# Scores padded to 128 rows with zeros, nearer softmax steps in one layer, and a key projection placed ahead of an output projection

## The reference, cut to what matters

```python
# layer A, one chunk: the stabilizer m_t enters every decay
d = b[..., :, None] - b[..., None, :] + ib[..., None, :]
m_t = jnp.maximum(inter, jnp.max(d, axis=-1))
p = jnp.einsum("bhtd,bhsd->bhts", qb, kb) * jnp.exp(d - m_t[..., None])
# layer B: a head has 128 columns without and 64 with rotary position
QK_HEAD = QK_NOPE + QK_ROPE        # 128 + 64
# the cross attention of the second block
kv = (mem_n @ w_ckv).reshape(B, M, 2, CROSS_HEADS, CROSS_HEAD_DIM)
s = jnp.einsum('bshd,bmhd->bhsm', q, k) * CROSS_HEAD_DIM ** -0.5
```

## Time and profile before

| | |
|---|---|
| median of 3 runs | 1611.77 us (1610.45 to 1612.25) |
| the profiled execution | 1605.89 us, span of its records 1604.1 us |
| instructions | 19197 |
| TensorE busy | 1552.2 us, 97% |
| mean granted clock of TensorE | 0.993 of full speed |

### The profile page before, as it was taken

One profiled execution on the slowest core, in us unless ns is written; L12 is line 12 of the kernel. 1 busy time (PEld: TensorE's weight loads), 2 busy tenths in 40 slices (PEclk: granted clock), 3 DMA queues, 4 the chain that ended last, 5 costly groups with the idle time before them and its releaser, 6 DMA issues.

```text
span 1604.1 us, 19197 instructions
## 1 busy us (share of the span) xinstructions
PE 1552.2 (97%) x7128; PEld 1239.7 (77%) x7128; DVE 890.2 (55%) x1775; ACT 705.5 (44%) x1607; POOL 192.1 (12%) x157
## 2 busy tenths in 40 slices
PE   7999999999999999999899999999999999999997
PEld 5887777777897877766478878688777888888886
DVE  6467485656465567556448557664455534444343
ACT  6544353333355666555334444442344333333241
POOL 3202020202120000000014004320001100000001
PEclk9999999999999999999999999999999999999998
DMA  5522122323424222121123321234322333333321
GB/s 191 158 74 72 53 80 66 92 66 118 125 67 143 81 62 61 49 71 42 40 79 120 92 67 55 65 105 120 99 84 79 95 103 93 101 96 93 105 93 65
DMA packets 89068, 141.04 MB, mean 88 GB/s; under 512 B 6416, under 2 KB 36496, under 8 KB 88976
## 3 DMA queue, kind: packets, MB, share of 16 engines
q1 hardware_dynamic: 88256, 139.02, 28.5%
q10 hardware_dynamic: 720, 0.81, 0.1%
HBM read 137.71 MB, written 2.10 MB: 87 GB/s over the span
## 4 chain that ended last, share of the span: by engine, by line
PE 78%; DVE 9%; ACT 5%; issue 3%; POOL 3%; DMA 2%; SPq 0%; POOLq 0%; ACTq 0%; DVEq 0%
PE banks L1242 16%; PE banks L1244 16%; PE banks L1243 16%; PE banks L1247 6%; PE banks L1249 6%; PE banks L1248 6%; PE banks L1205 2%; DVE sb_w_split L1927 2%; DVE sb_arena L1936 2%; ACT sb_junk L1512 2%; PE banks L1420 1%; PE banks L1405 1%; PE banks L1368 1%; ACT sb_w_split L1544 1%; DVE sb_arena L1927 1%
## 5 line engine op out<-in xcount | busy, mean ns | idle before, releaser
L1927 DVE TENSOR_TENSOR sb_w_split<-sb_raw,sb_w_split 128x512 fp32r<-128x512 f32 (+4 forms) x530 | 338.7, 681 | 359.8 <-ACT sb_w_split L1544 359.1
L1544 ACT ACTIVATE sb_w_split<-sb_raw 128x512 fp32r<-128x512 f32 (+4 forms) x530 | 288.2, 592 | 425.3 <-PE banks L1244 309.5
L1242 PE MATMUL banks<-sb_actA,sb_w_split 128*128 128x512 f32 x672 | 275.7, 410 | 0.3 <-ACT sb_arena L1604 0.3
L1244 PE MATMUL banks<-sb_actA,sb_w_split 128*128 128x512 f32 x672 | 262.7, 391 | 0.0
L1243 PE MATMUL banks<-sb_actA,sb_w_split 128*128 128x512 f32 x672 | 261.8, 390 | 0.0
L1242 PE MATMUL banks<-sb_actB,sb_w_split 128*128 128x512 f32 (+1 forms) x640 | 248.8, 389 | 4.2 <-DVE sb_actB L1927 2.2
L1244 PE MATMUL banks<-sb_actB,sb_w_split 128*128 128x512 f32 (+1 forms) x640 | 242.9, 379 | 0.0
L1243 PE MATMUL banks<-sb_actB,sb_w_split 128*128 128x512 f32 (+1 forms) x640 | 242.7, 379 | 0.0
L1247 PE MATMUL banks<-sb_w_split,sb_actA 128*128 128x512 f32 (+1 forms) x384 | 153.5, 400 | 12.6 <-DVE sb_w_split L1927 9.2
L1249 PE MATMUL banks<-sb_w_split,sb_actA 128*128 128x512 f32 (+1 forms) x384 | 149.3, 389 | 0.0
L1248 PE MATMUL banks<-sb_w_split,sb_actA 128*128 128x512 f32 (+1 forms) x384 | 149.0, 388 | 0.0
(11 more groups left out here) (206 smaller groups left out, 2061.4 us busy)
## 6 DMA issues: line engine op xcount, KB each, us to landing
sb_raw<-in_a_w_in SPq DMA_DIRECT2D x66, 256.0 KB, 3.0
sb_raw<-in_w_up SPq DMA_DIRECT2D x32, 512.0 KB, 3.6
sb_raw<-in_w_down SPq DMA_DIRECT2D x32, 512.0 KB, 3.7
sb_raw<-in_w_in SPq DMA_DIRECT2D x24, 512.0 KB, 3.6
sb_raw<-in_mem_w_kv SPq DMA_DIRECT2D x16, 512.0 KB, 3.8
sb_raw<-in_w_ckv SPq DMA_DIRECT2D x16, 512.0 KB, 3.7
sb_raw<-in_a_w_in SPq DMA_DIRECT2D x15, 512.0 KB, 3.8
sb_raw<-in_a_w_out SPq DMA_DIRECT2D x12, 512.0 KB, 3.9
```

The costliest lines, as they stand in the source:

```text
L1242: pe.op.matmul(out, hi[:, cs], x.hi(k), start=i == 0, stop=False)
L1244: t = pe.op.matmul(out, lo[:, cs], x.hi(k), start=False, stop=last_i)
L1544: act.op.activation(hi[:, cs], raw[:, cs], ACT.Copy).then_inc(act.mark(m("w_hi"), 2 * n + part + 1), 1)
L1927: dve.op.tensor_tensor(out, a, b, op).then_inc(dve.mark(*mark) if mark else dve.tick(), 1)
```

## The change

- `asc` and `hsc` take all 128 partitions. The rotary query of a head gets a tile of its own (`q_pe`), whose other half GpSimd sets to zero (in `prep4`); the stabilizer rows become 128 rows (`m_rows`), set to zero ahead of time, and the selector is used with its 128 rows. ScalarE copies the rotary queries in two halves.
- `mla` has `lag=1300`, `mem_b` `lag=1300, wait=1000`.
- `prep4` of the last pair comes only after the split of mixer tile 3, and the evictions of zB3 wait for the scores of head 3, since the new tiles lie where these were.
- ckD0 moves from behind outC1 to ahead of outC0; its result moves in the arena, and its evictions wait for the last pooling step. `dho` comes one group later, the loop has one group more, and cqD0 starts row by row.

```diff
--- before.py
+++ after.py
@@ -646,11 +646,11 @@
         rounds(0, [(h, j) for h in (h0, h0 + 1) for j in range(TT)], "asc", "atp",
                lambda u: [("aval", *u), ("ysplit", "yB", *u)], [("prep6", h0 // 2)],
                lambda u: [("silu", f"zB{u[0] // 2}", u[0] % 2)] + ([("ev", "quB3", 3)] if u[0] == B_HEADS - 1 else []),
-               lag=1400, wait=1000)
+               lag=1300, wait=1000)
 
     def mem_b(h0):
         rounds(0, [("B", h, i) for h in (h0, h0 + 1) for i in range(TT)], "msc", "mtp", lambda u: [("mval", *u)],
-               [("hnscale", "mqB"), ("hnt", "mk1", 3)], [("silu", f"mzB{h0 // 2}", 1)], lag=1600, wait=1200)
+               [("hnscale", "mqB"), ("hnt", "mk1", 3)], [("silu", f"mzB{h0 // 2}", 1)], lag=1300, wait=1000)
 
     def latents(q):
         if q == 3:
@@ -659,7 +659,8 @@
         p.need(("lat", "qlT", 2))
         p.product(f"quB{q}", [("prep6", q - 1)] if q else [])
         for n in range(7):
-            p.side(1, [("asc", 2 * q - 3, TT - 1)] if q >= 2 and n == 0 else (), (f"prep{n}", q), lag=4000 if n in (0, 6) else 2600)
+            after = [("asc", 2 * q - 3, TT - 1)] if q >= 2 and n == 0 else [("ysplit", "yB", 3)] if (q, n) == (3, 4) else ()
+            p.side(1, after, (f"prep{n}", q), lag=4000 if n in (0, 6) else 2600)
 
     def gated(name):
         p.product(name, (), lambda j: [(("silu", name, j),)])
@@ -708,7 +709,7 @@
     p.product("vC")
     units = [(h, j) for h in range(DIFF_HEADS) for j in range(TT)]
     turned, closing = None, []
-    for n in range(len(units) + 8):
+    for n in range(len(units) + 9):
         group, after, split = [], [("rtp", "q", 3)] if n == 0 else [], []
         for parts in closing:
             if len(parts) > 1:
@@ -720,7 +721,7 @@
             if turned[1] == TT - 1:
                 h = turned[0]
                 after = [("gateG", "gC4")]
-                closing.append([[("dhs", h)], [("dhr", h)], [("dho", h)], [("ysplit", "yC", 4 + h)]])
+                closing.append([[("dhs", h)], [("dhr", h)], [], [("dho", h)], [("ysplit", "yC", 4 + h)]])
             turned = None
         if 2 <= n < len(units) + 2:
             turned = units[n - 2]
@@ -742,17 +743,17 @@
         p.side(1, [("gateG", "gC0"), ("nrow", "m2"), ("dsc", g, TT - 1)], ("pp", g), *([("ysplit", "yC", g - 1)] if g else []))
     p.side(1, (), ("ysplit", "yC", POOL_GROUPS - 1))
     p.product("gC0", (), lambda j: [(("gateG", "gC0"),)] if j == 3 else [])
+    p.product("ckD0", [("nrow", "m2"), ("pw", POOL_GROUPS - 1)])
     p.product("outC0", first=False)
     p.product("outC1")
 
 
     p.put(("enter", "outC1"))
     scales(0, "d", after=[("sqp", "d", 7)])
-    p.product("ckD0")
     p.product("ckD1")
     p.rings = [(4, 5), (6, 7)]
     for g in range(2):
-        p.product(f"cqD{g}", [("nrow", "d")])
+        p.product(f"cqD{g}", [("nrow", "d")], first=g > 0)
         for n in (2 * g, 2 * g + 1):
             rounds(n % 2, [(n, i) for i in range(TT)], "csc", "ctp", lambda u: [("cval", *u)], (),
                    [("ev", f"cvD{g}", MT - 1)])
@@ -875,8 +876,8 @@
         self.decay = at.take(2, SEQ)
         self.u_pad = at.take(4, CONV_W + SEQ)
         self.sigA = at.take(2, SEQ)
-        self.neg_m = self.arena[0:4, at.at:at.at + SEQ]
-        at.take(SEQ)
+        self.m_rows = at.take(SEQ)
+        self.neg_m = self.m_rows[0:4, :]
         self.y_tok = at.take(TT, M_DIM)
         flat = self.y_tok.rearrange("p a b -> p (a b)")
         self.gate_f = flat[:, 0:SEQ]
@@ -918,6 +919,8 @@
         self.v_pair = [at.take(TT, 2 * V_HEAD) for _ in range(3)]
         self.kpe = at.take(TT, QK_ROPE)
         self.zT = [two[:, 1, 0:2, :], at.take(2, SEQ), two[:, 1, 4:6, :], Layout(self.arena, ARENA - 2048).take(2, SEQ)]
+        other = [self.zT[3][:, 0, :], self.zT[3][:, 1, :], two[:, 0, 6, :], self.zT[1][:, 0, :]]
+        self.q_pe = [[self.peT[n % 2][:, 1, :], other[n]] for n in range(4)]
         mprob_b = two[:, 0, 0:2, :].rearrange("p a b -> p (a b)")
         self.pair_pe = Layout(self.arena, ARENA - 1024).take(2, TT, 2 * QK_ROPE)
         self.sigB = self.cons[:, CON["head_rows"]:CON["head_rows"] + SEQ].rearrange("p (a b) -> p a b", a=1)
@@ -967,9 +970,9 @@
         self.row["m2"] = self.cons[:, CON["head_rows"]:CON["head_rows"] + N_MEM]
         self.scratch["m2"] = two[:, 0, 3, 0:N_MEM + P]
         at = Layout(self.arena, N_LATE + SEQ + 8 * SEQ + 4 * SEQ + 4 * SEQ)
+        self.cqT = at.take(8, SEQ)
         self.ckT = at.take(KD, N_MEM)
         self.cv = at.take(MT, D_MODEL)
-        self.cqT = at.take(8, SEQ)
         self.cpT = [at.take(MT, SEQ), at.take(MT, SEQ)]
         at = Layout(self.arena)
         self.cprob = [at.take(3, N_MEM), at.take(3, N_MEM)]
@@ -1347,8 +1350,8 @@
             place, full = open_bank(step)
             pe.wait_ge(*m.emptied(("gateT",)))
             mb = v.bank(place, n=n)
-            pe.op.matmul(mb, v.con("head_rows", h * P, (h + 1) * P, M_HEADS), v.neg_m[:, si * P:SEQ],
-                         start=True, stop=False)
+            pe.wait_ge(m("m_zero"), 1)
+            pe.op.matmul(mb, v.con("head_rows", h * P, (h + 1) * P), v.m_rows[:, si * P:SEQ], start=True, stop=False)
             add_mask(mb[:, 0:P], 2).then_inc(full, 1)
             place, full = open_bank(step, 1)
             pe.wait_ge(m("qk"), 4 * h + 4)
@@ -1396,13 +1399,14 @@
             h, j = a
             p, hh, ke = h // 2, h % 2, (j + 1) * P
             nT, eT = v.nopeT[p % 2], v.peT[p % 2]
-            qs, hs = slice(j * P, (j + 1) * P), slice(hh * 64, hh * 64 + 64)
+            qs = slice(j * P, (j + 1) * P)
             place, full = open_bank(step)
             for s in (0, 1, 3, 4, 5, 6):
                 pe.wait_ge(*m.emptied((f"prep{s}", p)))
             s = v.bank(place, n=ke)
             pe.op.matmul(s, nT[:, 2 + hh, qs], nT[:, hh, 0:ke], start=True, stop=False)
-            pe.op.matmul(s, eT[hs, 1, qs], eT[hs, 0, 0:ke], start=False, stop=False)
+            pe.wait_ge(m("q_fill"), (2, 4, 5, 6)[p])
+            pe.op.matmul(s, v.q_pe[p][hh][:, qs], eT[:, 0, 0:ke], start=False, stop=False)
             add_mask(s[:, j * P:], 3).then_inc(full, 1)
         elif kind == "atp":
             h, j = a
@@ -1792,9 +1796,13 @@
                         square(src[:, i, hh * width:(hh + 1) * width], sums[:, 2 * i + hh:2 * i + hh + 1],
                                m.at("sums", step) if last else None)
             if s != 2:
-                dst = {0: nT[:, 2, :], 1: nT[:, 3, :], 3: nT[:, 0, :], 4: nT[:, 1, :], 5: eT[:, 0, :], 6: eT[:, 1, :]}[s]
+                dst = {0: nT[:, 2, :], 1: nT[:, 3, :], 3: nT[:, 0, :], 4: nT[:, 1, :], 5: eT[:, 0, :]}.get(s)
                 src, place, empty = bank(step)
-                if s < 5:
+                if s == 6:
+                    act.wait_ge(m("q_fill"), (2, 4, 5, 6)[p])
+                    act.op.activation(v.q_pe[p][0][0:64, :], src[0:64, :], ACT.Copy).then_inc(act.tick(), 1)
+                    t = act.op.activation(v.q_pe[p][1][64:P, :], src[64:P, :], ACT.Copy)
+                elif s < 5:
                     t = act.op.activation(dst, src, ACT.Copy, scale=v.col("q_gain_nope" if s < 2 else "k_gain_nope"))
                 else:
                     t = act.op.activation(dst, src, ACT.Copy)
@@ -1891,10 +1899,14 @@
         return waits
     if kind == "quB":
         return [m.full(("prep6", q - 1)), m.at("qp", ("prep5", q - 1))] if q else [m.full(("lat", "qlT", 2))]
+    if name == "zB3":
+        return [m.full(("asc", 3, TT - 1))]
     if name == "zB2":
         return [m.full(("msc", "B", MEM_HEADS - 1, TT - 1))]
     if name == "mv1":
         return [m.product("mv1")]
+    if name == "ckD0":
+        return [m.at("pooled", ("pw", POOL_GROUPS - 1))]
     if name == "uC":
         return [m.at("rot", ("rot", "k", TT - 1))]
     if kind == "up" and name[-2] != "0":
@@ -2121,6 +2133,7 @@
             dve.op.tensor_tensor_scan(g[3], g[1], g[1], 0.0, ALU.max, ALU.max).then_inc(dve.tick(), 1)
         elif kind == "gateA":
             dve.settle()
+            dve.wait_ge(m("m_zero"), 1)
             scalar(v.neg_m, g[3], -1.0, ALU.mult)
             dve.settle()
             tensor(g[4], v.neg_m, g[6], ALU.subtract, *m.at("g_m", step))
@@ -2482,12 +2495,26 @@
             pool.op.tensor_tensor(u[:, 16:], mean, u[:, 16:], ALU.subtract).then_inc(pool.tick(), 1)
             pool.settle()
             pool.op.tensor_tensor(u[:, 0:16], edge, u[:, 0:16], ALU.subtract).then_inc(pool.mark(*m.at("pooled", step)), 1)
+        elif kind == "prep4":
+            n = a[0]
+            if n < 2:
+                for sem, value in pair_free(m, 0) + pair_free(m, n) + [m.full(("msc", "A", MEM_HEADS - 1, TT - 1))]:
+                    pool.wait_ge(sem, value)
+                pool.op.memset(v.q_pe[n][0], 0.0).then_inc(m("q_fill"), 1)
+            elif n == 2:
+                pool.wait_ge(*m.full(("msc", "B", MEM_HEADS - 1, TT - 1)))
+            else:
```

(5 more changed lines are left out.)

## The result

The changed kernel takes 1587.74 us (median of 4 runs, 1586.50 to 1590.15) against 1611.11 (4 runs, 1609.57 to 1612.25) in the same comparison: ratio 0.9857, 95% interval 0.984 to 0.9874, 23.4 us less. The profiled execution took 1587.57 us, 18.3 less than the one of before (1605.89). So of the 9.1 us that were not foreseen some 4 are between the two profiles and some 5 are not: they lie in how the profiled execution of before stood to its median.

The account below looks back on a forecast made before the run. TensorE's own stream (97% busy) plus its few waits was taken as the bound. Terms -13.1 (zero-filled scores), +1.0 (given back), -2.2 (distances) and 0 (ckD0) gave -14.3 us: 1605.89 to 1591.6, median 1597.5, range 1590 to 1606.

Parts of the forecast that it names:

- I make the sum against the profiled one and carry that difference to the median.: Whole kernel: savings are taken from the profiled 1605.89 us, then its 5.88 us distance to the median is added back.
- the wait of 3.05 at 734 stays: Layer B, where four memory tiles are split as outB0 starts: TensorE's 3.05 us wait was expected to remain.
- -2.2 for the shorter distances: End of layer B: three of seven forced rounds move earlier, removing head 6's waits of 0.66 and 1.58 us.
- Zero-filled scores: TensorE's stream: 32 rotary tiles save 0.27 us each, 16 stabilizer tiles 0.28, together 13.1; 1.0 given back in forced rounds.
- rival A: TensorE's short matmuls: only their longer records are saved, 4.5 us; total -5.7, 1606.1 us; chance 0.08.
- rival B: Matmuls beside the mask: surplus stays whatever their rows, so only waits gain, -2.2, 1609.6 us; chance 0.04.
- What the zeros cost: GpSimd's seven memsets (3.2 us) and ScalarE's split query copies (2.4 us): costed at nothing, since both engines have idle time.
- Rival E: At 720 to 740 us GpSimd's late zeros hold up ScalarE and its weight splits: slower, 1615 us; chance 0.03.
- ckD0, right in sum: Second block's mixer end: moving ckD0 removes 1.2 us of small waits, a possible second stall costs 1.2; net 0.
- rival D: Layer B's denser rounds cost 4 us and ckD0's new place a second stall of 4: -6.3, 1605.5 us; chance 0.15.
- C: Waits vanish more widely, with rounds to spare once they begin earlier: -21.4, 1590.4 us; chance 0.15.
- both lower bounds of the waits: Best cases: -5.3 for the distances if the wait at 734 goes too, -5.2 for ckD0's new place.

Follow-up runs that it names:

- filled_waits: Kernel before with 98 throw-away bf16 matmuls placed in five TensorE waits of heads 4, 6 and 7 in layer B: 1605.1 us, ratio 0.9956.
- undo_near: Changed kernel with the old distances of layer B (1400 and 1000, 1600 and 1200): 1596.9 us, ratio 0.9915.
- rows_no_zero: Kernel before with line 1405 over all 128 rows, without zeros, memsets or waits, so outputs mix two heads: 1602.4 us, ratio 0.9951.

## Why the prediction was wrong

**The step that failed first: "I make the sum against the profiled one and carry that difference to the median."** The 5.88 us were taken as a constant. They were time at 1.2 GHz behind waits at the end of layer B, which the profiled execution mostly lacked and the two further ones had (1.7 us lost there against 10.2); and the change takes it away in part (3.4 lost). The mean clock rises from 0.9884 to 0.9925, worth 4.7 us by the slope between runs and 6.7 by the product. In the changed kernel profile and median are 0.17 apart. filled_waits shows that the clock alone can bring as much. The sum had no term for the clock in layer B.

**The second: "the wait of 3.05 at 734 stays", and -2.2 for the shorter distances.** It went, and with it, as forecast, the two of head 6 (0.66 and 1.58, in undo_near 0.96 and 1.65); waits of 1.07 and 1.97 came in their place. Those of the last head were
```profile
791.68 0.44 PE L1205 MATMUL banks<-sb_cons,sb_arena 128*128 128x128 f32 x2 [0.88 <-DVE sb_arena L1930]
796.91 0.66 PE L1205 MATMUL banks<-sb_cons,sb_arena 128*128 128x128 f32 x4 [2.38 <-DVE sb_arena L1930]
```
in the kernel before and are 1.44 and 2.16 now, 0.3 more together. Measured without the clock the distances bring 5.5 to 7.6 us on the changed kernel, where 2.2 was forecast. The count of rounds was off by one: three stay forced, where four were forecast to stay. On the kernel before, the memory attention's distances alone bring 0.5 to 2.6 at full clock. Why the step is worth more beside the zeros, and where its last 2.5 us lie, stays open. The self-attention's own distance may have a part: by the plan it moves nearly nothing alone, but beside the memory attention's it puts some scores up to five steps earlier, and no run has it by itself.

**Zero-filled scores, right.** 13.1 less 1.0 given back was forecast; undo_near, which is this part with ckD0's, measures 10.9 to 12.1 us without the clock, and the two parts alone 10 to 12. The records (593 ns), the loads and the tile (1.74 us, 1.77 forecast) are as stated. The stabilizer's share stands alone in layer A, which takes 436.4 us before and 430.2 now, 434.7 and 430.2 less the lost time: 4.5, as forecast. (0.08 + 0.21 is 0.29 and not 0.28, which changes the sum by 0.2.) The lower bound of rival A (4.5) and rival B's zero are out; B's end was also that of the Trainium skill's "TensorE: Matmul & The Clock Gate", section "Why this matters for your kernels", whose rule is on a lone matmul with K=32; in this stream it doesn't carry over, since the 4-row record took 640 ns and its 128-row form 592.

**What the zeros cost, right.** About 1 us at most (rows_no_zero). Rival E did not occur: in 720 to 780 only transposes wait (line 1208), all for DVE.

**ckD0, right in sum.** Forecast 0; alone it measured -0.5 to +0.5 us, in the changed kernel -0.7 to +0.9. DVE's wait for POOL and the stall behind outC1, now at the start of cqD0, are both there; the second stall that rival D feared came at 1000.78 with 2.25, from ACT, in place of the 1.8 of the earlier trace rows. The other half of D, a loss by denser rounds, came only at distances nearer than those of the change.

**The rivals.** C named the direction, waits vanish more widely, and 1590.4 us, with a chance of 0.15. Its mechanism was half the truth: the wait at 734 went, but the list of PE's waits fell by only 2.6 us in all. The clock, which no rival held, and what the distances gained outside the listed waits did the rest. So C's figure lies near the result in part by luck. No bound helped either: with both lower bounds of the waits (3.1 and 5.2 us more) the sum ends at 1589.2, still above 1587.7.

By the mean times (1611.5 to 1588.0, 23.5 us less) the accounts are: zeros 11 to 12, distances 6 to 6.6, clock 5 to 7, ckD0 nothing.

## What to carry to other kernels

Before one profiled execution is used as the base of a sum, compare its mean granted clock with that of the timed runs; where they differ, as 0.993 and 0.988 did here, the difference between profile and median can be a cost with a place, and an edit nearby can remove it. In a stream of 128-row fp32 products a 64- or 4-row product cost more than its zero-padded form, about 0.25 us each here (11 to 12 us in 48); padding pays as long as another engine has time for the zeros. Move dependent rounds nearer only as far as the engines behind them follow: of the settings tried 1300 was best, 1000 was level with it or a little behind, and 650 lost 18 us.

## What the runs showed of the hardware

Two executions of the same kernel with the same waits (3.05, 0.66 and 1.58 us in both) had different clocks behind them (1.00 and 0.72 in 738 to 745 us), so a wait of 3 us doesn't always bring the lower level; over 48 runs of the kernel the mean clock lay between 0.985 and 0.992, and the time moved by 1.16 us per 0.001. Filling 6 us of PE's waits in layer B (20.0 to 14.0 us) with useless matmuls gained 5.7 us. Such a fill in the changed kernel took the lower level out of layer B (3.4 us lost before it, none after) and gained nothing that the runs can tell. In layer B of the kernel before, a 64-row record of 512 columns took 641 ns and its weight load began after 0.76 us of idle load side; with 128 rows it is 593 ns and 0.24.
